# Gate/up products of a SwiGLU layer by Strassen's scheme: seven block products for eight, with weight sums on GpSimd and product sums on VectorE

## The reference

```python
h = rms_norm(x, g_mix)
z = h @ w_in                  # q, k, v, ssm input, two gates
a_out = dilated_attention(q, k, v, g_q, g_k) @ w_attn_proj
s_out = (y @ w_glu_a) * sigmoid(y @ w_glu_b)       # y = gelu(s5_ssm(u, ...))
x = x + (sigmoid(gate_a) * a_out + sigmoid(gate_s) * s_out) @ w_out
h2 = rms_norm(x, g_ffn)
x = x + (silu(h2 @ w_ffn_gate) * (h2 @ w_ffn_up)) @ w_ffn_down
```

## Time and profile before

| | us |
|---|---|
| median of 3 runs | 881.95 (880.73 to 882.22) |
| profiled execution, its own time | 880.76 |
| its span, first to last instruction | 879.0 |
| TensorE busy | 868.8 |
| VectorE busy | 457.6 |
| ScalarE busy | 322.9 |
| GpSimd busy | 151.7 |

### The profile page before, as it was taken

How to read it: one execution, slowest core, us unless ns; L and a number is a source line. 1 busy time by engine, 2 the same in 40 slices (tenths; PEclk the granted TensorE clock), 3 DMA queues, 4 the chain that set the end, 5 groups by cost and what they waited for, 6 DMA issues and landing times.

```text
span 879.0 us, 13174 instructions
## 1 busy us (share of the span) xinstructions
PE 868.8 (99%) x4627; PEld 715.5 (81%) x4627; DVE 457.6 (52%) x638; ACT 322.9 (37%) x488; POOL 151.7 (17%) x207
## 2 busy tenths in 40 slices
PE   9999999999999999999999999999999999999998
PEld 7788788888887887877887888888888888888886
DVE  5558976677914453543586563333334444433334
ACT  6322343323246656655433342222222222322221
POOL 3789995100020000001220230000000000000000
PEclk9999999999999999999999999999999999999999
DMA  8439237634465442322635333333333232222222
GB/s 303 144 108 228 88 126 143 213 119 143 136 194 182 144 150 88 124 62 76 170 119 192 96 97 95 97 95 95 95 95 95 95 95 96 96 96 95 95 72 95
DMA packets 86082, 108.82 MB, mean 124 GB/s; under 512 B 10688, under 2 KB 51888, under 8 KB 85920
## 3 DMA queue, kind: packets, MB, share of 16 engines
q1 hardware_dynamic: 79136, 94.24, 34.0%
q10 hardware_dynamic: 5504, 10.52, 3.7%
q0 software_dynamic: 1408, 3.61, 1.9%
HBM read 94.38 MB, written 13.96 MB: 123 GB/s over the span
## 4 chain that ended last, share of the span: by engine, by line
PE 52%; DVE 2%; issue 1%; ACT 0%; DVEq 0%; ACTq 0%
PE ps L1517 27%; PE ps L1547 13%; PE ps L1243 11%; DVE late L1225 1%; DVE late L1145 0%; DVE w_lo L557 0%; DVE hT_lo L1151 0%; PE ps L1436 0%; ACT w_hi L551 0%; ACT late L721 0%; PE ps L1422 0%; PE ps L1532 0%; DVE late L1076 0%; DVE late L1148 0%; PE ps L1527 0%
## 5 line engine op out<-in xcount | busy, mean ns | idle before, releaser
L557 DVE TENSOR_TENSOR w_lo<-w_raw,w_hi 128x1024 fp32r<-128x1024 f32 x141 | 178.3, 1265 | 321.0 <-ACT w_hi L551 320.9
L551 ACT ACTIVATE w_hi<-w_raw 128x1024 fp32r<-128x1024 f32 x141 | 149.3, 1059 | 396.1 <-PE ps L1243 162.0
L1517 PE MATMUL ps<-h_hi,w_hi 128*128 128x512 f32 x352 | 137.2, 390 | 0.0
L1517 PE MATMUL ps<-h_hi,w_lo 128*128 128x512 f32 x352 | 137.0, 389 | 0.0
L1517 PE MATMUL ps<-h_lo,w_hi 128*128 128x512 f32 x352 | 136.9, 389 | 0.0
L1243 PE MATMUL ps<-w_hi,hT_hi 128*128 128x512 f32 x280 | 109.8, 392 | 1.8 <-DVE w_lo L557 1.1
L1243 PE MATMUL ps<-w_lo,hT_hi 128*128 128x512 f32 x280 | 109.0, 389 | 0.0
L1243 PE MATMUL ps<-w_hi,hT_lo 128*128 128x512 f32 x280 | 109.0, 389 | 0.0
L414 POOL TENSOR_TENSOR early<-early 128x16 f32<-128x16 f32 (+6 forms) x129 | 91.3, 708 | 23.1 <-ACT early L574 13.1
L1243 PE MATMUL ps<-hT_hi,w_hi 128*128 128x512 f32 x224 | 91.5, 408 | 0.0
L1243 PE MATMUL ps<-hT_hi,w_lo 128*128 128x512 f32 x224 | 87.7, 391 | 0.0
(11 more groups left out here) (212 smaller groups left out, 1103.2 us busy)
## 6 DMA issues: line engine op xcount, KB each, us to landing
w_raw<-in_w_in SPq DMA_DIRECT2D x108, 256.0 KB, 3.5
w_raw<-in_w_ffn_gate SPq DMA_DIRECT2D x44, 256.0 KB, 2.8
w_raw<-in_w_ffn_up SPq DMA_DIRECT2D x44, 256.0 KB, 3.0
w_raw<-in_w_ffn_down SPq DMA_DIRECT2D x44, 256.0 KB, 2.8
z_d<-early ACTq DMA_DIRECT2D x7, 1024.0 KB, 4.8
late<-z_d SPq DMA_DIRECT2D x96, 64.0 KB
w_raw<-in_w_out SPq DMA_DIRECT2D x16, 256.0 KB, 3.0
late<-z_d SPq DMA_DIRECT2D x12, 256.0 KB
```

The costliest lines, as they stand in the source:

```text
L551: nc.scalar.activation(w_hi[:, j % WSPL], w_raw[:, j % WRAW], ACT.Copy).then_inc(w_hi_done, 1)
L557: nc.vector.tensor_tensor(w_lo[:, j % WSPL], w_raw[:, j % WRAW], w_hi[:, j % WSPL].bitcast(F32), ALU.subtract).then_inc(w_lo_done, 1)
L1517: ins = T.matmul(ps[:, m], (w_hi, w_lo)[b][:, j % WSPL, at_w:at_w + P], (h2_hi, h2_lo)[a][:, 2 * j + h, :], start=j == 0 and h == 0 and k ...
```

## The change

Blocks 0 to 2 (`FP` = 3) stay as they are. In blocks 3 to 10, the product of a block is seen as a 2 x 2 block product: the columns are cut in two halves of 256 (each 128 gate and 128 up), the 1024 rows in two halves of 512, the tokens in `low` and `high` of 256. Strassen's scheme in Winograd's form gives the four output blocks from seven products instead of eight. Each product i has its own PSUM bank, `BANK[i]`, and is added up over two passes p; pass p uses weight tiles p and p + 2, and is called a unit.

- Weights: three of the seven weight operands of a pass are pieces of `w_raw`, four are sums of pieces, S1 to S4, which GpSimd makes into `sums_f` (`block_sums`). ScalarE rounds each of the seven (`op_hi`, 128 x 512) and VectorE makes its low part (`op_lo`). There is one slot for each operand: `op_hi` of a unit waits until TensorE has used that operand of the unit before.
- Activations: VectorE makes the normalized `hn` once (`normed`), GpSimd four differences of its blocks, and ScalarE and VectorE split all seven partners once (`partner_hi`, `partner_lo`), in the time of blocks 1 and 2. They lie in `hT_hi`/`hT_lo` and, once the third block has used them, in `h2_hi`/`h2_lo`.
- Matmuls: `seven(f)` does 2 passes x 7 products x 2 column groups x 2 row tiles x 3 matmuls, each of 128 x 128 weights on 256 tokens.
- Products: after the second pass ScalarE copies the bank of product 0 (`first_copied`), and VectorE makes C11, U2, U3, C21, U4, C22, C12 (`c11`, `c21`, `c22_c12`), each of one bank and one SBUF tile. ScalarE applies one Silu of 1024 elements (`gates_silu`), VectorE one multiplication (`gated_up`). Since `hn` is normalized already, the multiplication by `norm_all` falls away.
- TensorE's first pass of the next block waits, product by product, for the merge that read its bank.
- SP loads each tile by four DMAs of 128 KB in place of two of 256 KB, with column halves, row tiles and gate/up interleaved (`blocks`), and waits for the third low part and the fourth sum of the tile's unit (`tile_used`).
- The down stage begins with banks in another order, and its first two tiles are split ahead of its loop.
- The state space part has other start flags on some matmuls; their number and order stay.

```diff
+FP = 3
-W_DOWN = W_FFN + 4 * FB
+W_DOWN = W_FFN + 4 * FP
...
+        hn = s_raw[:, 2 * FP:2 * FP + 8]
+        t_raw = [s_raw[:, 2 * FP + 8 + 2 * n:2 * FP + 10 + 2 * n].rearrange("p m t -> p (m t)").rearrange("p (k t) -> p k t", k=4)
+                 for n in range(4)]
+        wx = [wx_t[:, n] for n in range(2)]
+        sums_f = [off(23552 + 512 * n, 512) for n in range(4)]
+        c_out = off(4096, 2048).rearrange("p (b g t) -> p b g t", b=4, g=2)
+        p1_f, u2_f, u3_f, u4_f = (off(6144 + 512 * n, 512) for n in range(4))
...
+        BANK = (4, 5, 6, 0, 1, 2, 3)
+        C_11, C_U2, C_U3, C_21, C_U4, C_22, C_12 = range(1, 8)
+        def unit(f, p):
+            return 2 * (f - FP) + p
+        def op_at(i, r):
+            if i < 4:
+                return (w_hi, w_lo)[r][:, i // 2, i % 2 * 512:i % 2 * 512 + 512]
+            return wx[r][:, (i - 4) * 512:(i - 3) * 512]
+        def partner(i, r):
+            if i in (0, 1, 6):
+                n = 2 + 2 * (0, 1, 6).index(i)
+                at = (hT_hi, hT_lo)[r][:, n:n + 2]
+            else:
+                at = (h2_hi, h2_lo)[r][:, 2 * (i - 2):2 * (i - 2) + 2]
+            return at.rearrange("p m t -> p (m t)").rearrange("p (k t) -> p k t", k=4)
+        def partner_raw(i):
+            if i in (0, 1, 6):
+                k, t0 = ((0, 0), (4, 0), (4, 256))[(0, 1, 6).index(i)]
+                return hn[:, k:k + 4, t0:t0 + 256]
+            return t_raw[{2: 3, 3: 0, 4: 2, 5: 1}[i]]
+        def op_raw(i, p):
+            if i < 3:
+                return w_raw[:, p + (0, 2, 2)[i], (0, 0, 512)[i]:(0, 0, 512)[i] + 512]
+            return sums_f[i - 3]
+        def tile_landed(f, j):
+            return 64 * (f - FP) + 8 * W_DOWN + (64 if j else 48)
...
-            with sp.Fori(0, FB) as f:
+            with sp.Fori(0, FP) as f:
...
+            def blocks(f, j):
+                for g, name in enumerate(("w_ffn_gate", "w_ffn_up")):
+                    for h in range(2):
+                        sp.dma_start(w_raw[:, j].rearrange("p (m h g c) -> p m h g c", m=2, h=2, g=2)[:, :, h, g],
+                                     t[name][(2 * j + h) * P:(2 * j + h + 1) * P, bass.ds(f * 256, 256)]
+                                     .rearrange("p (m c) -> p m c", m=2)).then_inc(raw_landed[j], 16)
+            def tile_used(f, j):
+                sp.wait_ge(op_lo_done, 7 * unit(f, j % 2) + 3)
+                sp.wait_ge(sum_done, 4 * unit(f, j % 2) + 4)
+            for j in range(4):
+                sp.wait_ge(w_lo_done, W_DOWN - WRAW + 1 + j)
+                blocks(FP, j)
+            with sp.Fori(FP + 1, FB) as f:
+                for j in range(4):
+                    tile_used(f - 1, j)
+                    blocks(f, j)
...
+            low, high = slice(0, 256), slice(256, 512)
+            pool.wait_ge(hn_done, KT)
+            for n, (a, b) in enumerate(((hn[:, 0:4, high], hn[:, 0:4, low]), (hn[:, 4:8, high], t_raw[0]),
+                                        (hn[:, 4:8, high], hn[:, 0:4, high]), (t_raw[1], hn[:, 4:8, low]))):
+                if n:
+                    pool.wait_ge(t_done, n)
+                pool.tensor_tensor(t_raw[n], a, b, ALU.subtract).then_inc(t_done, 1)
+            def block_sums(f, p, first=False):
+                u = unit(f, p)
+                pool.wait_ge(raw_landed[p], tile_landed(f, p))
+                pool.wait_ge(raw_landed[p + 2], tile_landed(f, p + 2))
+                a11, a21, a12, a22 = (w_raw[:, p + k, m:m + 512] for k in (0, 2) for m in (0, 512))
+                s1, s3, s2, s4 = sums_f
+                for n, (out, a, b, op) in enumerate(((s1, a21, a22, ALU.add), (s3, a11, a21, ALU.subtract),
+                                                     (s2, s1, a11, ALU.subtract), (s4, a12, s2, ALU.subtract))):
+                    if not first:
+                        pool.wait_ge(op_lo_done, 7 * u + n - 3)
+                    if n >= 2:
+                        pool.wait_ge(sum_done, 4 * u + n)
+                    pool.tensor_tensor(out, a, b, op).then_inc(sum_done, 1)
+            block_sums(FP, 0, True)
+            block_sums(FP, 1)
+            with pool.Fori(FP + 1, FB) as f:
+                for p in range(2):
+                    block_sums(f, p)
...
+            def partner_hi(i):
+                if i in (0, 1, 6):
+                    act.wait_ge(hn_done, KT)
+                else:
+                    act.wait_ge(t_done, {2: 4, 3: 1, 4: 3, 5: 2}[i])
+                    act.wait_ge(gemm_steps, 4 * (W_DOWN - 4 + i - 2) + 4)
+                nc.scalar.activation(partner(i, 0), partner_raw(i), ACT.Copy).then_inc(b_hi_done, 1)
+            def op_hi(f, p, i, first=False):
+                u = unit(f, p)
+                if not first:
+                    act.wait_ge(op_used, 7 * u + i - 6)
+                elif i < 4:
+                    act.wait_ge(gemm_steps, 4 * (W_DOWN - 1 + i // 2))
+                if i < 3:
+                    act.wait_ge(raw_landed[p + (0, 2, 2)[i]], tile_landed(f, p + (0, 2, 2)[i]))
+                else:
+                    act.wait_ge(sum_done, 4 * u + i - 2)
+                nc.scalar.activation(op_at(i, 0), op_raw(i, p), ACT.Copy).then_inc(op_hi_done, 1)
+            def first_copied(f, first=False):
+                act.wait_ge(op_used, 7 * unit(f, 1) + 1)
+                if not first:
+                    act.wait_ge(c_steps, 7 * (f - FP) - 7 + C_U2)
+                nc.scalar.activation(p1_f, ps[:, BANK[0]], ACT.Copy).then_inc(p1_copied, 1)
+            def gates_silu(f):
+                act.wait_ge(c_steps, 7 * (f - FP) + C_12)
+                nc.scalar.activation(c_out[:, :, 0], c_out[:, :, 0], ACT.Silu).then_inc(c_silu, 1)
+            def half_a(f, first=False):
+                for i in range(7):
+                    op_hi(f, 1, i)
+                    if i == 2 and not first:
+                        gates_silu(f - 1)
+            def half_b(f, first=False):
+                for i in range(7):
+                    op_hi(f + 1, 0, i)
+                    if i == 1:
+                        first_copied(f, first)
...
             silus(0, 2)
+            silus(1)
+            for j in range(1, 4):
+                hi(W_FFN + j + 8, j)
+                partner_hi((0, 1, 6)[j - 1])
+            for i in (2, 3, 4):
+                partner_hi(i)
+            for i in (0, 1):
+                op_hi(FP, 0, i, True)
+            for m in range(2):
+                act.wait_ge(ffn_evac, 8 + m + 1)
+                nc.scalar.activation(sg[:, m], sg[:, m], ACT.Silu).then_inc(silu_done, 1)
+            for i in (2, 3):
+                op_hi(FP, 0, i, True)
+            partner_hi(5)
+            for i in (4, 5, 6):
+                op_hi(FP, 0, i, True)
+            half_a(FP, True)
+            half_b(FP, True)
+            with act.Fori(FP + 1, FB - 1) as f:
+                half_a(f)
+                half_b(f)
+            half_a(FB - 1)
...
+            def normed(k):
+                V.scalar_tensor_tensor(out=hn[:, k], in0=x1[:, k], scalar=gffnT[:, k:k + 1], in1=norm_all[:, :],
+                                       op0=ALU.mult, op1=ALU.mult).then_inc(hn_done, 1)
+            n_partner = [0]
+            def partner_lo(i):
+                n_partner[0] += 1
+                dve.wait_ge(b_hi_done, n_partner[0])
+                V.tensor_tensor(partner(i, 1), partner_raw(i), partner(i, 0).bitcast(F32), ALU.subtract).then_inc(b_lo_done, 1)
+            def op_lo(f, p, i):
+                dve.wait_ge(op_hi_done, 7 * unit(f, p) + i + 1)
+                V.tensor_tensor(op_at(i, 1), op_raw(i, p), op_at(i, 0).bitcast(F32), ALU.subtract).then_inc(op_lo_done, 1)
+            blk = lambda b: c_out[:, b].rearrange("p g t -> p (g t)")
+            def merged(f, step, out, i, other, op=ALU.add, needs=0):
+                dve.wait_ge(op_used, 7 * unit(f, 1) + i + 1)
+                if needs:
+                    dve.wait_ge(c_steps, 7 * (f - FP) + needs)
+                a, b = (other, ps[:, BANK[i]]) if op == ALU.subtract else (ps[:, BANK[i]], other)
+                V.tensor_tensor(out, a, b, op).then_inc(c_steps, 1)
+            def c11(f):
+                dve.wait_ge(s_raw_done, 2 * f)
+                dve.wait_ge(p1_copied, f - (FP - 1))
+                merged(f, C_11, blk(0), 1, p1_f)
+            def c21(f):
+                merged(f, C_U2, u2_f, 5, p1_f)
+                merged(f, C_U3, u3_f, 4, u2_f, needs=C_U2)
+                merged(f, C_21, blk(2), 2, u3_f, ALU.subtract, needs=C_U3)
+            def c22_c12(f):
+                merged(f, C_U4, u4_f, 3, u2_f)
+                merged(f, C_22, blk(3), 3, u3_f)
+                merged(f, C_12, blk(1), 6, u4_f, needs=C_U4)
+            def gated_up(f):
+                dve.wait_ge(c_silu, f - (FP - 1))
+                V.tensor_tensor(s_raw[:, bass.ds(2 * f, 2)].rearrange("p m (t x) -> p (m t) x", t=2), c_out[:, :, 0], c_out[:, :, 1],
+                                ALU.mult).then_inc(s_raw_done, 2)
```

(146 more changed lines are left out.)

11 lines of the change are left out of this document (7 added, 4 removed).

## The result

The changed kernel takes 895.53 us (median of 4 runs, 893.79 to 896.48) against 881.34 for the kernel before on the same chip: 1.016 times, 95% interval 1.0145 to 1.0176. It is 14.2 us slower, where 8.5 us faster was predicted, and lies outside the predicted range of 862 to 888.

What follows compares the result with a forecast made beforehand. The prediction took the matmul stream as the bound: eight blocks' 174.0 us become 155.9, less 9.1 us of stalls and 0.5 at the switch, so 8.5 us faster, 873.4 us on the median's scale; range 862 to 888.

Steps and rivals of the forecast that it cites:

- m: Time per 256-column matmul in the seven-product blocks: 116 ns taken, between bounds of 111.8 and 120.
- L1393's 111.8 ns: Time per matmul read from an existing 128-column fp32 row, where load and stream overlap; taken as the lower bound.
- Rival A: Seven-product blocks: matmuls cheap (111.8 ns) and stalls small (0.3 us), 21.6 us less, 860; chance 0.14.
- The new wait: TensorE waits at product 3 for VectorE's C22: 1.3 us at each of seven block boundaries, 9.1 us; bounds 0 and 2.5.
- VectorE's load: VectorE's work per seven-product block: 14.2 us alone, 19 to 21 us with GpSimd's sums beside it; near-critical.
- The price of a meeting: In seven-product blocks, a VectorE low part that meets a GpSimd sum costs 0.6 us more; PSUM merges keep 0.69.
- the prologue and switch: Plain blocks 1 and 2 cover the preparation; the change to seven-product blocks costs 0.5 us.
- the tiles' loop: Tile 2's loads behind tile 1's, through landing, sums and merges: 19.8 us against a period of 20.6, fits by 0.8.
- the stall is at product 0 or 2 and comes from a landing: One of the signs named in advance, at block boundaries, that would show the prediction wrong.
- The sum: Whole kernel: 174.0 - 155.9 - 9.1 - 0.5 = 8.5 us less, giving 873.4 us.
- D: Nothing measurable: matmuls at 120 ns and stalls of 1.5 to 2 us, under 1 us less; chance 0.09.
- B: VectorE and GpSimd become the bound through their shared port: at 22.7 us per block 7.6 us more, 890; chance 0.16.

Runs made afterwards that it cites:

- e2: The changed kernel with the four activation differences made by VectorE in place of GpSimd: 893.25 us, 1.0133 times the kernel before.
- e3: The changed kernel with GpSimd's 64 weight sums touching only one column each (output not the reference's): 871.01 us, 0.9882 times the kernel before.
- e7: e6 with GpSimd's first two sums of a block's second half also waiting for low part 5: 875.35 us, 0.994 times the kernel before.
- e1: The changed kernel with SyncE loading a block's tiles in the order 0, 2, 1, 3: 885.04 us, 1.0042 times the kernel before.
- e4: The changed kernel with VectorE making U4 and C22 ahead of low part 6: 896.44 us, 1.0173 times the kernel before.
- e5: The changed kernel with the edits of e1 and e4 together: 880.88 us, 0.9997 times the kernel before.
- e8: e6 with all 64 weight sums on VectorE, GpSimd idle: 870.13 us, 0.9873 times the kernel before.
- e9: The changed kernel with only its 64 weight sums moved to VectorE: 908.47 us, 1.0313 times the kernel before.
- e11: e9 with the tile order 0, 2, 1, 3: 873.73 us, 0.9916 times the kernel before.
- e6: e5 with normalized activations and their four differences made by VectorE early, in plain block 1: 878.14 us, 0.9969 times the kernel before.
- e10: The kernel before with each 512-column gate/up matmul issued as two of 256: 894.89 us in one run, against 880.83 beside it.

## Why the prediction was wrong, step by step

- *What bounds the kernel*: right. The loss and all later gains are in the matmul stream's waits and intervals.
- *m*: the upper bound was right. 226.5 and 120 ns differ by 106.5 for 256 columns, within 0.2 ns the stream at 2.4 GHz, so the 13.3 ns beside the columns are the same at both sizes. Every matmul here has its own load, so no run says whether they belong to it. L1393's 111.8 ns did not carry over. The mean of 116 cost 1344 x 4 ns = 5.4 us. Rival A's condition was wrong with it.
- *The new wait*: place, releaser and order were as predicted for product 3, plus a second wait at product 2, ended by C21. Its size, 1.4 us per boundary, is near the 1.3 predicted, but partly by luck: m of 120 covers more of the chain, and the meetings were dearer.
- *VectorE's load*: seven sums of 0.69 are 4.8 us, not 4.6, a slip of 0.2. The estimate of 19 to 21 us per block was near: it is busy for 85.27 of 100 us (640 to 740), 18.6 us per block.
- *The price of a meeting*, "a low part that meets a sum costs 0.6 us more", was mis-sized. I had scaled the 2.31 us of a 1024-wide operation down to 512. What is added looks like the rest of GpSimd's instruction, so a 512-wide low part goes from 0.69 to as much as 1.78 us, 1.1 more, and a 1024-wide one beside a 1024-wide difference to 3.4, 2.2 more. e2, e3 and e7 show it by taking the meetings away.
- *The step that failed* is the prologue and switch, "I charge 0.5 us", with the tiles' loop, "it fits by 0.8 us". Together they cost 16.3 us at the places that happen once (2.2, 3.1, 8.8 and 2.2 of clock). The prediction's own sign for this, "the stall is at product 0 or 2 and comes from a landing", is what the first boundary shows, and its 8.8 us lie far over the stall's upper bound of 2.5. I worked the loop out for the steady period and did not walk it through the first block. There GpSimd's sums could start only at 590.86, when VectorE was through with low part 3, and VectorE's burst at the switch then held them back, so that tile 1 was loaded only from 601.41 on and tile 2 behind it from 603.60, landing at 608.04. e1 takes 10.5 us off by the order of four loads. Even in steady state the loop left no room, since the merge order of e4 gained nothing until e5 mended the tile order. One of its terms was also too small: a tile's four issues take 2.19 us (603.60 to 605.79), 0.55 each and not 0.47, so eight take 0.6 us of the 0.8 us by which it was to fit.
- *The sum*: from 8.5 us less to the 13.1 more of the profiled execution is 21.6 us: 5.4 by m, 1.0 less at the boundaries (8.1 for 9.1), 15.8 at the places that happen once (16.3 for 0.5), and 1.4 after waits.
- *The rivals*: D came nearest in its conditions (m 120, 1.4 us per boundary) and gives no change; the loss is what it leaves out, the places that happen once. B named the right pair of engines for the wrong reason. It is not their rate, since VectorE keeps up at 95% in e8 and, with the sums on GpSimd, at 99% in e7; it is latency in two loops, which e9 and e11 separate from the engine's load. That TensorE would lose its clock after a wait stood nowhere.

What stays open: the 3.5 us at the first boundary in e5 and e6 (2.4 in e7) were not taken apart further, but they are absent in e8 and e11, where GpSimd makes no sums. A second wait at the switch, 1.6 us between starts in e8, e9 and e11 and 1.9 to 2.0 in the others with full-length sums but e2, was not taken apart either. That VectorE's burst is what delayed GpSimd at the first boundary is read from the durations below; no run moves the burst alone.

## What to carry to other kernels

Before counting matmul columns saved, take the interval of two starts at the new size from its fixed part: halving 512 columns costs 53% of the interval, not 50, and Strassen's eighth becomes a fourteenth. A loop through several queues (low part, load order, landing, sum, merge) must be walked through its first round, with each queue's order written out, and mending one loop shows nothing while another sets the period. And work moved to GpSimd is not free for VectorE: here the sums cost more beside it (875.35 us in e7) than on it (870.13 in e8).

## What the runs showed of the hardware

VectorE's operations with two SBUF operands and GpSimd's seem to take turns by whole instructions. In the changed kernel at 590.61 us VectorE came with seven such operations back to back, all at full speed, and GpSimd's two sums beside them took 6.98 us in place of 2.56:

```profile
590.86 6.98 POOL L640 TENSOR_TENSOR late<-w_raw 128x512 f32<-128x512 f32 x2 [6.12 <-DVE w_lo L1388]
```

```profile
590.61 1.21 DVE L1384 TENSOR_TENSOR h_lo<-late,h_hi 128x1024 fp32r<-128x1024 f32 x1
591.75 1.88 DVE L1388 TENSOR_TENSOR wx_t<-late,wx_t 128x512 fp32r<-128x512 f32 x3
593.55 1.88 DVE L1388 TENSOR_TENSOR w_lo<-w_raw,w_hi 128x512 fp32r<-128x512 f32 x3
```

At 701.60 both are slowed: two low parts take 3.48 us in place of 1.28, and GpSimd's pair beside them, from 702.79, takes 3.44 in place of 2.56. That they take turns is read from these durations; no run isolates it. The Trainium skill (GPSIMD Engine Reference, § Specifications) has the two share SBUF interfaces and says that VectorE instructions with two SBUF inputs contend; the trace agrees and adds the price. The Trainium skill's formula for the gap between two isolated matmuls (TensorE: Matmul & The Clock Gate, § Back-to-back issue gap) gives 109.2 ns at 256 columns; e10 measures 120.

The same wait doesn't always cost the clock. At the first boundary e5 waits 3.47 us between starts and runs 14 intervals of 213 or 214 ns after it; e6 waits 3.49 and runs none.
